# Two-layer decoder trunk on one core: conditioning pieces on the weight queue, more buffers for them, and a later compression tail

## What is computed

```python
mod = (cond @ w_ada[l] + b_ada[l])[:, None, :]          # cond = silu(c), one row
sh1, sc1, g1, sh2, sc2, g2 = jnp.split(mod, 6, axis=-1)
h = rmsnorm(x, norm_g[l, 0]) * (1.0 + sc1) + sh1
proj = h @ w_in[l]                                       # pooling, queries, 6 key/value parts, gates
a_out = pool_mixer(...)                                  # 4 windows, 4 small products
o_out = nsa_mixer(...)                                   # compressed, selected and sliding attention
x = x + g1 * (jnp.concatenate([a_out, o_out], axis=-1) @ w_out[l])
h2 = rmsnorm(x, norm_g[l, 1]) * (1.0 + sc2) + sh2
gate, up = jnp.split(h2 @ w_gate_up[l], 2, axis=-1)
x = x + g2 * ((jax.nn.silu(gate) * up) @ w_down[l])
```

## Time and profile before

| | |
|---|---|
| median of 3 runs | 2325.27 us (2321.72 to 2327.61) |
| profiled execution, its own time | 2325.14 us |
| its span, first to last instruction | 2323.3 us |
| PE / DVE / ACT / POOL busy | 2158.4 / 1636.1 / 1002.0 / 202.9 us |
| mean granted clock of PE | 0.975 |

### The profile page before, as it was taken

The page is one execution under the profiler, slowest core; times in us unless marked ns, Lnnn a source line. Parts: engine busy times, 40 slices in busy tenths (PEclk is TensorE's granted clock), DMA queues, the critical chain, the costliest instruction groups (busy, mean ns, idle before and its releaser), DMA issues.

```text
span 2323.3 us, 26303 instructions
## 1 busy us (share of the span) xinstructions
PE 2158.4 (93%) x9820; PEld 1765.9 (76%) x9820; DVE 1636.1 (70%) x2394; ACT 1002.0 (43%) x1464; POOL 202.9 (9%) x388
## 2 busy tenths in 40 slices
PE   2678998688999999999998999998999999999999
PEld 1467786467888888888886877787888888888887
DVE  6977978758767888788786677465975545555555
ACT  3333654253434444443444446545443444444343
POOL 3201111101101111111110010000100000000000
PEclk9889999889999999999999999999999999999999
DMA  9968878748858888888884685443975555555554
GB/s 397 395 242 304 283 266 316 280 160 318 313 187 312 313 325 319 315 315 321 316 308 162 234 299 191 179 166 143 346 278 199 182 195 188 197 182 198 188 193 145
DMA packets 110492, 590.70 MB, mean 254 GB/s; under 512 B 12448, under 2 KB 13088, under 8 KB 63904
## 3 DMA queue, kind: packets, MB, share of 16 engines
q1 hardware_dynamic: 54640, 386.56, 45.7%
q0 software_dynamic: 55296, 201.35, 23.1%
q10 hardware_dynamic: 432, 1.13, 0.1%
HBM read 586.89 MB, written 2.10 MB: 254 GB/s over the span
## 4 chain that ended last, share of the span: by engine, by line
PE 73%; DVE 11%; DMA 8%; issue 5%; ACT 2%; POOL 0%; DVEq 0%; ACTq 0%; POOLq 0%
PE ps L462 23%; PE ps L467 23%; PE ps L466 23%; DMA ada<-w_ada 7%; DVE w_lo L1191 3%; DVE ada L1215 3%; PE ps L765 1%; DMA qT<-w_ada 1%; PE ps L630 1%; ACT w_hi L861 1%; PE ps L662 1%; PE ps L489 1%; PE ps L705 1%; PE ps L716 1%; PE ps L573 0%
## 5 line engine op out<-in xcount | busy, mean ns | idle before, releaser
L1191 DVE TENSOR_TENSOR w_lo<-raw,w_hi 128x1024 fp32r<-128x1024 f32 x704 | 846.5, 1222 | 380.1 <-ACT w_hi L861 379.5
L861 ACT ACTIVATE w_hi<-raw 128x1024 fp32r<-128x1024 f32 x704 | 734.9, 1057 | 719.9 <-PE ps L467 676.5
L462 PE MATMUL ps<-w_hi,h_hi 128*128 128x512 f32 x1920 | 776.8, 405 | 33.5 <-DVE w_lo L1191 23.0
L467 PE MATMUL ps<-w_hi,h_lo 128*128 128x512 f32 x1920 | 757.6, 395 | 0.0
L466 PE MATMUL ps<-w_lo,h_hi 128*128 128x512 f32 x1920 | 757.2, 394 | 0.0
L462 PEld LDWEIGHTS ps<-w_hi,h_hi 128*128 128x128 f32 x1920 | 367.0, 191 | 118.0 <-issue 33.6
L466 PEld LDWEIGHTS ps<-w_lo,h_hi 128*128 128x128 f32 x1920 | 366.6, 191 | 79.7 <-issue 5.5
L467 PEld LDWEIGHTS ps<-w_hi,h_lo 128*128 128x128 f32 x1920 | 365.8, 191 | 78.4
L462 PE MATMUL ps<-w_hi,a_hi 128*128 128x512 f32 x896 | 356.4, 398 | 3.8 <-ACT w_hi L861 1.3
L467 PE MATMUL ps<-w_hi,a_lo 128*128 128x512 f32 x896 | 349.3, 390 | 0.0
L466 PE MATMUL ps<-w_lo,a_hi 128*128 128x512 f32 x896 | 348.9, 389 | 0.0
(11 more groups left out here) (166 smaller groups left out, 1069.4 us busy)
## 6 DMA issues: line engine op xcount, KB each, us to landing
raw<-stream SPq DMA_DIRECT2D x360, 1024.0 KB, 4.9
ada<-w_ada POOLq DMA_DIRECT2D x338, 512.0 KB, 5.7
qT<-w_ada POOLq DMA_DIRECT2D x12, 512.0 KB, 13.0
gate<-w_ada POOLq DMA_DIRECT2D x10, 512.0 KB, 13.0
raw<-stream SPq DMA_DIRECT2D x4, 896.0 KB, 6.7
kT<-w_ada POOLq DMA_DIRECT2D x6, 512.0 KB, 13.1
val<-w_ada POOLq DMA_DIRECT2D x6, 512.0 KB, 13.3
uc<-w_ada POOLq DMA_DIRECT2D x6, 512.0 KB, 13.7
```

Of the source, the lines that this page charges most:

```text
L462: mm = pe.matmul(bank[:], xh, whi[s][:, k, :], start=begin, stop=False)
L467: mm = pe.matmul(bank[:], xl, whi[s][:, k, :], start=False, stop=end)
L861: act.activation(whi[h % 4][:].rearrange("p k c -> p (k c)"), raw[t % 4][:, a * 1024:(a + 1) * 1024], ACT.Copy).then_inc(hi_ready.sem, 1)
L1191: dve.tensor_tensor(wlo[h % 4][:].rearrange("p k c -> p (k c)"), raw[t % 4][:, a * 1024:(a + 1) * 1024], whi[h % 4][:].rearrange("p k c -> ...
```

## The change

1. Pieces 64 to 383 are no longer loaded by POOL but by SP, which loads the weight tiles, in one hand-written order: at tile `t` first weight tile `t + 4`, then the pieces that follow into the buffers of that period's sums, then weight tiles whose buffer a direct tile frees late (`FREED_LATE`). POOL keeps the first 64.
2. From piece 139 (summed at tile 45 of layer 0) to piece 319, nine buffers instead of three: the six added are borrowed from attention, whose work is over by then.
3. `ROOM` of layer 0 is new: of pieces 64 to 88, more are summed at tiles 12 to 19.
4. The compression tail (`hidden_turn`, `cmp_out`, `take_cmp`, `kcmp_turn`, first compressed scores) comes one tile later in both layers.
5. The staging of the norms goes from DVE to ACT in both layers.
6. At tile 12 the split of the gate weights comes first on ACT and DVE.

```diff
 M_USE = ordered(
-    [(0, 0, "kv"), (14, 0, "hidden"), (23, SIDE, "hidden turned"), (23, MID, "cmp out"),
-     (26, MID, "cmp scores 0"), (29, MID, "cmp scores 1")]
+    [(0, 0, "kv"), (14, 0, "hidden"), (24, SIDE, "hidden turned"), (24, MID, "cmp out"),
+     (27, MID, "cmp scores 0"), (29, MID, "cmp scores 1")]
...
-ROOM = ({10: 3, 11: 3, 12: 4, 15: 4, 17: 4, 19: 3, 21: 1, 23: 1, 24: 2, 25: 2, 26: 1, 27: 2}
-        | {t: 3 for t in ATT_SPLIT if t >= 28} | {45: 4, 47: 4, 49: 4},
+ROOM = ({10: 3, 11: 1, 12: 6, 15: 6, 17: 5, 19: 4, 21: 1, 23: 2, 24: 1, 25: 2, 26: 1, 27: 1, 28: 3, 29: 2, 30: 3}
+        | {t: 3 for t in ATT_SPLIT if t >= 31} | {34: 2, 38: 2},
...
+ADA_LATE = min(q for (layer, t), qs in ADA_SUMS.items() if layer == 0 and t >= 45 for q in qs)
+ADA_LAST = min(q for (layer, t), qs in ADA_SUMS.items() if layer == 1 for q in qs)
+RING, LATE_RING = (0, 1, 2), (3, 4, 5, 7, 0, 1, 2, 6, 8)
...
+        elif ADA_LATE <= q < ADA_LAST:
+            s = LATE_RING[(q - ADA_LATE) % len(LATE_RING)]
+        else:
+            s = RING[q % len(RING)]
...
+ADA_NEXT = {before: q for q, (_, _, before) in enumerate(ADA_SLOT)}
+FREED_LATE = {12: (13, 14), 15: (16,), 17: (18,), 19: (20,), 24: (22,), 34: (32,), 39: (37,)}
...
+            def load_ada(q):
+                s, _, before = ADA_SLOT[q]
+                sp.wait_ge(ada_summed.sem, before + 1)
+                sp.dma_start(ada_buf[s], w_ada[q]).then_inc(ada_landed[s].sem, 16)
+
+            for n in range(4):
+                load(n)
+            for layer in range(DEPTH):
+                here.layer = layer
+                for t in range(TILES):
+                    if t not in DIRECT and layer * TILES + t + 4 < DEPTH * TILES:
+                        load(layer * TILES + t + 4)
...
+                    for q in ADA_SUMS.get((layer, t), ()):
+                        if ADA_NEXT.get(q) is not None:
+                            load_ada(ADA_NEXT[q])
+                    for d in FREED_LATE.get(t, ()):
+                        load(layer * TILES + d + 4)
+                    if layer == 0 and t == 43:
+
+                        sp.wait_ge(bank_s.full.sem, bank_s.full.at(here, S_USE[f"scores {NSTEP - 1}"] + 1))
+                        for i in range(4):
+                            load_ada(ADA_LATE + i)
...
         def _(pool):
-            for q, (s, _, before) in enumerate(ADA_SLOT):
+            for q, (s, _, before) in enumerate(ADA_SLOT[:FIRST_HALVES]):
...
                 for i, t in enumerate((*T_Q0, *T_Q1)):
-                    if t == 23:
+                    if t == 24:
                         hidden_turn()
-                    if t == 24:
                         stage_turn(bank_a, A_USE["q 0"], ST_Q0, 0, 4)
                         stage_turn(bank_b, B_USE["q 0"], ST_Q0 + 1, 1, 4)
-                    if t == 25:
-                        kcmp_turn()
...
+                    if t == 26:
+                        kcmp_turn()
...
+                def stage(j):
+                    for tok in range(TOKS):
+                        last = act.activation(bufb[:, j % 2, tok * 256:(tok + 1) * 256],
+                                              x[:, tok, j * 256:(j + 1) * 256], ACT.Copy, scale=rs[:, tok:tok + 1])
+                    last.then_inc(norm_staged.sem, 1)
+
+                act.wait_ge(rs_ready.sem, rs_ready.at(here, which))
+                stage(0)
+                stage(1)
...
-                if t == 23:
+                if t == 24:
                     take_cmp()
```

More of the change, by code:

```diff
@@ L195, with ada_slots @@
 ADA_SUMS = ada_schedule()
+ADA_LATE = min(q for (layer, t), qs in ADA_SUMS.items() if layer == 0 and t >= 45 for q in qs)
+ADA_LAST = min(q for (layer, t), qs in ADA_SUMS.items() if layer == 1 for q in qs)
+RING, LATE_RING = (0, 1, 2), (3, 4, 5, 7, 0, 1, 2, 6, 8)
+def ada_slots():
+    last, out = {}, []
+    for q in range(len(ADA)):
+        if q < FIRST_HALVES:
+            s = q % ADA_SLOTS
+        elif ADA_LATE <= q < ADA_LAST:
+            s = LATE_RING[(q - ADA_LATE) % len(LATE_RING)]
+        else:
+            s = RING[q % len(RING)]
+        n, before = last.get(s, (0, None))
+        out.append((s, n, before))
+        last[s] = (n + 1, q)
+        if q == FIRST_HALVES - 1:
+            last = {s: (0, b) for s, (_, b) in last.items()}
+    return out
+ADA_SLOT = ada_slots()
+ADA_NEXT = {before: q for q, (_, _, before) in enumerate(ADA_SLOT)}
+FREED_LATE = {12: (13, 14), 15: (16,), 17: (18,), 19: (20,), 24: (22,), 34: (32,), 39: (37,)}
+assert sorted(t for ts in FREED_LATE.values() for t in ts) == sorted(DIRECT)
 SCALE_GROUPS = [g for g in range(len(ADA) // GROUP) if ADA[g * GROUP].vec in (SC1, SC2)]
@@ L346, in build @@
         raw_free = [count(f"raw_free{s}", TILES // 4, PART_TILES // 4) for s in range(4)]
-        ada_landed = [count(f"ada_landed{s}") for s in range(ADA_SLOTS)]
+        ada_first = [count(f"ada_first{s}") for s in range(ADA_SLOTS)]
+        ada_landed = [count(f"ada_landed{s}") for s in range(len(LATE_RING))]
         first_landed = count("first_landed")
@@ L401, in _, with load @@
             flat = stream.rearrange("l t p c -> (l t) p c")
-            for n in range(DEPTH * TILES):
+            def load(n):
                 s, cols = n % 4, tile_cols(n % TILES)
@@ L410, in _ @@
                 sp.dma_start(raw[s][:, 0:cols], flat[n, :, 0:cols]).then_inc(raw_landed[s].sem, 16)
+            def load_ada(q):
[9 more added lines that the diff above has]
+                        load(layer * TILES + t + 4)
+                    if layer == 0 and t == 9:
+                        for q in range(FIRST_HALVES, FIRST_HALVES + ADA_RING):
+                            load_ada(q)
+                    for q in ADA_SUMS.get((layer, t), ()):
[7 more added lines that the diff above has]
+                            load_ada(ADA_LATE + i)
+                    if layer == 0 and t == 45:
+                        sp.wait_ge(bank_b.full.sem, bank_b.full.at(here, B_USE["heads 3"] + 1))
+                        for i in (7, 8):
+                            load_ada(ADA_LATE + i)
             rows = out.rearrange("(q p) d -> p q d", p=P)
@@ L484, in norm_turn @@
                 pe.wait_ge(bank.free.sem, bank.free.at(here, uses[f"norm{which} {j}"]))
-                pe.wait_ge(stage_ready.sem, stage_ready.at(here, (ST_NORM1 if which == 1 else ST_NORM2) + j + 1))
+                pe.wait_ge(norm_staged.sem, norm_staged.at(here, 8 * (which - 1) + j + 1))
                 for k in range(2):
@@ L1255, in rstd @@
                     dve.wait_ge(dve_step.sem, step())
-                    dve.scalar_tensor_tensor(v if i == 2 else y, e, 1.5, y, ALU.add, ALU.mult)\
-                        .then_inc(dve_step.sem, 1)
-                    dve.wait_ge(dve_step.sem, step())
+                    last = dve.scalar_tensor_tensor(v if i == 2 else y, e, 1.5, y, ALU.add, ALU.mult)
+                    if i == 2 and done is not None:
+                        last.then_inc(done.sem, 1)
+                    else:
+                        last.then_inc(dve_step.sem, 1)
+                        dve.wait_ge(dve_step.sem, step())
             def norm(which, t0):
@@ L1264, in norm @@
                 dve.wait_ge(dve_step.sem, step())
[L1265 to L1281 removed]
+                rstd(rs[:], D, rs_ready)
                 first = which == 1 and here.layer == 0
@@ L1510, in period @@
                         heads_to_rows(u)
-                if nxt is not None:
-                    split_lo(nxt, 0)
                 if t == 12:
@@ L1516, in period @@
                         .then_inc(gl_lo.sem, 1)
-                if t == 27:
+                if nxt is not None:
+                    split_lo(nxt, 0)
+                if t == 28:
                     cmp_scale(0)
```

58 lines of the change are left out of this document (18 added, 40 removed).

## The result

The changed kernel takes 2337.7 us (median of 6 runs, 2333.97 to 2341.08), the kernel before 2326.99 us beside it (6 runs). The ratio is 1.005, 95% interval 1.0037 to 1.0064: slower by 0.5%. The profiled execution has a span of 2335.1 us, 11.8 us more than before.

What follows compares the result with a forecast made beforehand. The prediction took PE's gaps outside 590 to 1200 us as what could pay, with DVE setting the late pace; its terms, -13.5 - 7.2 + 9.3 + 6.7 + 2.0 + 1.9 = -0.8, took 2325.1 to 2324.3 us, range 2296 to 2337.

Steps and rivals of the forecast that it cites:

- second rival: PE stalls behind every weight tile that stands behind a sum on SP's list: 2338.8 us, chance 0.18.
- C: Layer 0, tiles 12 to 26: waits removed, but late weight tiles and the later tail cost +9.3 us, bounds -5 and +13.
- D: Layer 0, weight tiles 36 and 41 behind the sums of periods 34 and 39: +6.7 us, bounds 0 and +9.
- E: Layer 1, hidden row's wait goes but weight tile 26 comes late: +2.0 us, bounds -4.3 and +5.
- F: Norms of both layers, staging on ACT instead of DVE: +1.9 us, bounds -1 and +4.
- A: Nine buffers from piece 139 on, DVE's waits from 366 to 470 us go: -13.5 us, bounds -7 and -18.6.
- B: Pieces in the MLP's first part, 570 to 590 us: waits and low clock go, -7.2 us, bounds -5.5 and -7.2.
- C up to tile 24: Layer 0 from tile 12: 10.1 us of gaps removed and 10.1 us of losses cancel, bounds -5 and +4.
- C at tile 26: Layer 0, weight tile 26 issued only after `take_cmp` and a sum, so the probabilities' turn is late: +9.3 us.
- the walk: The prediction's step-by-step timing of sums, weight tile issues, landings (6.1 us taken) and ACT work up to PE's turns.
- third rival: Nine buffers don't take the waits away, DMA is late in bursts and A gives half: 2331 us, chance 0.12.
- Moving the loads to SP by itself: Piece loads from POOL to SP: costed at nothing, hidden by asking a sum's time ahead; otherwise 1.3 us a piece.

Runs made afterwards that it cites:

- e2: The changed kernel with the late-freed weight tiles issued ahead of that period's pieces on SP instead of behind them: 2311.1 us, ratio 0.994.
- e6: e2 with the `ROOM` table of sums of the kernel before: 2299.43 us, ratio 0.9882.
- e10: The changed kernel with the `ROOM` table of before, pieces still ahead of the late-freed weight tiles: 2333.93 us, ratio 1.0023.
- e1: The changed kernel with all pieces issued by POOL again, same order and waits, nine late buffers kept: 2323.53 us, ratio 0.9978.
- e12: e6 with its pieces issued by POOL in place of SP: 2308.96 us, ratio 0.9921.
- e9: The kernel before with only the nine buffers from piece 139 on, pieces still issued by POOL: 2312.41 us, ratio 0.9938.
- e13: e6 with three buffers for the late pieces as before, instead of nine: 2311.27 us, ratio 0.9931.
- e3: The changed kernel with the staging of the norms back on DVE: 2340.43 us, ratio 1.0062.

## Why the prediction was wrong

2324.3 us was forecast and 2337.7 measured, outside 2296 to 2337 and on the slower side. The mechanism of the second rival, *one queue holds the weight tiles back*, given 0.18 and priced at 2338.8 us, is what happened; e2 shows it. My forecast had the same mechanism and sized it too small. That the rival's price came within 1.1 us is luck. It had C, D and E at 27 us, and they came to 40.1; it had 4 for F and 3.4 for the clock on top, and only 20.7 of gain, where A and B gave 27.6. It also wanted landings near 9.5 us, and those of its three tiles in layer 0 were 7.0, 5.5 and 7.1: it's the asking that was late.

**C up to tile 24: the step that failed first.** C as a whole was +9.3 with a bound of +13, and came to +17.5. "Up to tile 24 gains and losses cancel": they came to +8.8 us (tile 10 to 23). The 10.1 us of waits did go. The wait at tile 17 is 6.12, where I had 2.4: tile 17 landed at 186.1 as walked (185.4), but it was asked for behind sum 73 and PE, 6.1 us early at tile 15, was there at 182.5, not 185.3. I had moved PE by the 3.2 us of the logits alone; in before the logits behind that gap also start slowly, 0.41 us each in place of 0.28, at a granted clock of 0.87 from 167 to 180 us against 1.00 in the changed kernel. Tile 17 took 7.0 us to land, issued right behind the six pieces, far from the 12.6 (4.8 + 7.8) that the bound by the order of one queue allowed. Then tiles 19 and 21 lose 4.1 and 5.3 more, where I gave 2.9 for all. With the old table and tiles first (e6) the stretch gains 3.3 us; the table is some 8 to 10 us of it (e2 against e6, changed kernel against e10; 16.8 with the pieces on POOL, e1 against e12), the order 2 to 4. I had priced the table as four sums, 4.8 us, and missed that every sum more ahead of a load also delays the load.

**C at tile 26** was +9.3; measured +8.7 (7.7 to 16.4). Issue at 248.7, landing 5.5 us later and 3.6 us on ACT are the walk, with all of it 7 us later because of the stretch ahead.

**D** was +6.7; from tile 28 (17.2 us late) to tile 41 (28.6) the kernel lost 11.4 us, 4.7 of it at 36 (2.1 was given without a walk) and 7.2 at 41 (4.6), above its bound of 9. e1 and e2 lose nothing at tile 41. The moment was right: SP asks for weight tile 41 at 375.15, which less the 21.4 us that the kernel is late there is 353.8, where the walk had 354.3. It landed 7.1 us later in place of 6.1, and the turn stands at 386.23. The step that was left out is what PE does after the stall: four matmuls of the turn take 1.09 us as a group where they took 0.60, and tile 41 itself starts 3.5 us behind its turn in place of 1.8. The stretches behind the stalls ahead of tile 41 and tile 26 in the changed kernel, and behind the same turn of tile 41 in before (columns of the earlier trace rows):

```profile
386.00:390.00 4.00, 3.77 (x15) 3.28 (x15) 4.00 (x6) 1.63 (x3) 0.00 (x0) 0.50 0.02 6
257.50:261.00 3.50, 3.26 (x9) 2.69 (x10) 3.50 (x9) 3.50 (x22) 0.00 (x0) 0.50 0.17 35
```

```profile
359.00:361.50 2.50, 2.50 (x18) 1.96 (x16) 2.50 (x5) 1.49 (x2) 0.00 (x0) 1.00 1.08 447
```

PE comes out of these two stalls at a granted clock of 0.50, the lower of its two levels (1.2 of 2.4 GHz). The forecast charged that only to B.

**E** was +2.0; measured +11.2 at tile 26 of layer 1, the largest error of a term, and outside its bound of 5. The 4.25 us at the hidden row did mostly go (1.36 are left). The walk had `cmp_out` end at 1368.0; it ended at 1373.3. I had left out that weight tile 24 is itself late behind sums: ACT waited 6.12 us for it, until 1365.4, and tile 24 started at 1369.3 where the walk had 1363.9. The remainders of tile 25's split stand ahead of `take_cmp` on DVE (another 1.1 us, 1374.4), its sums ended at 1380.9, where I had 1374.5, and the landing took 7.7 us in place of 6.2, behind two pieces asked for in the 1.6 us ahead of it.

**A** was -13.5; tiles 41 to 51 gained 22.7, and the second norm gave 3.5 back: -19.2, a little more than the far bound. The early three waits went too. But nine buffers alone give 7.8 there (e9), and in the best version 11.3 of its 17.9 (e13); on POOL that version gains 12.1 there (e12), so the issuer is a part too. The changed kernel's 22.7 are more than either; that DVE came there with its own work done while PE was late is likely, and not shown. The 3.5 us at the norm are the table's, whose last three sums moved to tile 51; I had not priced them. The third rival, half of A, was right for POOL (e9) and not for SP.

**B** was -7.2; measured -8.4, 1.2 us past its bound, and -7.5 in e9: right in cause and nearly in size.

**F** was +1.9; no loss shown (e3). The sign of the estimate wasn't supported: up to the first tile of layer 0 staging on ACT even gains 1.3 us, and the second norm loses as much with it (3.5) as without (3.6).

The sum by its own steps, as measured: start and first norm -1.1, C +8.8 and +8.7, tile 26 to 28 +0.8, D +11.4, A -19.2, B -8.4, norm and first tiles of layer 1 up to tile 25 -1.4, E +11.2, rest +1.0: +11.8 us of span.

Moving the loads to SP by itself was costed at nothing. It isn't nothing, either way: with the weight tiles behind the pieces it is 14 us slower than POOL (e1), with the tiles ahead 9.5 to 12 us faster (e12, and e2 against e1). The term compared landings of unequal sizes. Pieces of equal size land in 3.03 us at the shortest in the changed kernel and 3.42 in before, from 160 us on, and SP asks 0.27 us sooner after the sum.

What stays open: how much of the changed kernel's gain from tile 41 to 51 is only DVE catching up while PE was late was not tried by itself. Nor was the order of the weight tiles among themselves: the hand-written list puts 27 ahead of 26, and with the late tail 28 too, and in e1 and e12, with nothing else on SP, tile 26 of layer 0 still starts 7.7 and 5.3 us later against before than tile 25 does.

## What to carry to other kernels

When two kinds of transfers are put on one in-order list, the waits of one become waits of the other: for each load, ask which semaphore the entry *ahead* of it waits for, and when that comes in the new kernel, not in the old one. Put the transfer whose landing gates the critical engine first; here this swap of two loops made a 0.5% loss into a 0.6% gain, and with the old table 1.2%. A walk that carries old times into the new order underestimates, because lateness feeds the sums on which the next loads wait: when several such waits have no slack in the walk, take the upper bounds together, and charge each long stall for the PE clock behind it as well, where the trace shows it fall.

## What the hardware showed that was not expected

A piece of 512 KB landed sooner when SP issued it than when POOL did: from 160 us on the shortest is 3.03 to 3.17 us in the runs with pieces on SP and 3.33 to 3.43 in those on POOL (before, e1, e9, e12).

Weight tile 41, asked for at 349.4 in e6 and e12, lands after 7.8 us when the pieces asked for behind it are on the same queue, and after 10.2 when they come from POOL's. That is one place and no rule for a longer stretch: from 340 to 450 us the weight tiles land in a median of 9.1 us in e6 and 7.9 in e12 (least, median and most, e6 first, then e12):

```profile
DMA to landing us min/median/max: 5.6/9.1/12.6
```

```profile
DMA to landing us min/median/max: 5.5/7.9/10.2
```

In that stretch the two kernels move 355 and 329 GB/s, with the DMA busy 0.93 and 0.87 of the time; whether the slower kernel moves less because of its queues, or because it is slower, isn't shown:

```profile
340.00:450.00 110.00, 91.95 (x407) 70.75 (x405) 104.09 (x170) 42.42 (x73) 0.00 (x0) 0.98 0.93 355
```

```profile
340.00:450.00 110.00, 91.69 (x385) 70.06 (x384) 95.08 (x156) 39.16 (x67) 23.69 (x45) 0.94 0.87 329
```
